# A retention gate by seven block products, head norms squared on ScalarE, tokens in turn through the up-projection, and a weight sum done by an adding DMA

## The reference, cut to what matters

```python
u = rmsnorm(h, norm_mix[l])
q, k, v, g_ret, p, gates = jnp.split(u @ w_in[l], split_points, axis=-1)
q, k = rotary(q), rotary(k) * 256 ** -0.5
ret = retention(q, k, v)                       # 4 heads of 256
ret = ret * lax.rsqrt(jnp.mean(ret * ret, axis=-1, keepdims=True) + NORM_EPS)
ret = ret.reshape(b, s, RET_V) * jax.nn.silu(g_ret)
pool_out = multiscale_pool(p, pool_w[l], pool_scale[l])
gate = jax.nn.sigmoid(gates.reshape(b, s, 2, D_MODEL) + gate_bias[l])
merged = gate[:, :, 0] * (ret @ w_ret_up[l]) + gate[:, :, 1] * (pool_out @ w_pool_up[l])
h = h + merged @ w_out[l]
```

## Time and profile before

| what | us |
|---|---|
| median of 3 runs | 1188.58 (1188.36 to 1188.71) |
| the profiled execution | 1188.89 |
| its span, first to last instruction | 1187.2 |
| TensorE busy in the span | 1177.9 (99%) |
| VectorE busy | 951.2 (80%) |
| ScalarE busy | 690.2 (58%) |
| GpSimd busy | 168.3 (14%) |

### The profile page before, as it was taken

The page is one execution under the profiler, slowest core; times in us unless marked ns, Lnnn a source line. Parts: engine busy times, 40 slices in busy tenths (PEclk is TensorE's granted clock), DMA queues, the critical chain, the costliest instruction groups (busy, mean ns, idle before and its releaser), DMA issues.

```text
span 1187.2 us, 14701 instructions
## 1 busy us (share of the span) xinstructions
PE 1177.9 (99%) x5704; PEld 976.9 (82%) x5704; DVE 951.2 (80%) x1158; ACT 690.2 (58%) x827; POOL 168.3 (14%) x170
## 2 busy tenths in 40 slices
PE   9999999999999999999999999999999999999997
PEld 8777888888888888888888888888899888888886
DVE  7788798878778798878788887569997766988884
ACT  7775656656547666554565555657562445566642
POOL 2100132210200132120031220000000100222200
PEclk9999999999999999999999999999999999999999
DMA  9434565447343555555455555652784344555540
GB/s 342 173 132 159 185 246 182 177 177 272 132 142 104 216 198 189 184 210 200 155 193 196 214 213 171 253 210 86 245 306 172 136 159 175 197 200 182 188 173 36
DMA packets 32872, 221.96 MB, mean 187 GB/s; under 512 B 3777, under 2 KB 4289, under 8 KB 7074
## 3 DMA queue, kind: packets, MB, share of 16 engines
q1 hardware_dynamic: 32514, 219.77, 51.4%
q0 software_dynamic: 144, 1.05, 0.5%
q10 hardware_dynamic: 144, 0.20, 0.0%
HBM read 219.95 MB, written 1.05 MB: 186 GB/s over the span
## 4 chain that ended last, share of the span: by engine, by line
PE 98%; issue 1%; DVE 1%; DMA 0%; ACT 0%; SPq 0%; POOLq 0%; POOL 0%; DVEq 0%; ACTq 0%
PE ps L305 30%; PE ps L307 30%; PE ps L306 30%; PE ps L310 5%; PE ps L313 3%; DMA raw<-in_w 0%; ACT whi L257 0%; DVE h L472 0%; DVE AR L2829 0%; DVE st L1878 0%; SPq L2851 0%; DVE AR L1896 0%; DVE AR L2477 0%; ACT whi L274 0%; ACT AR L2820 0%
## 5 line engine op out<-in xcount | busy, mean ns | idle before, releaser
L264 DVE SCALAR_TENSOR_TENSOR wlo<-raw,whi 128x2048 fp32r<-128x2048 f32 x164 | 375.2, 2295 | 75.7 <-ACT whi L257 48.4
L257 ACT CAST whi<-raw 128x2048 fp32r<-128x2048 f32 x166 | 317.7, 1916 | 172.0 <-PE ps L307 164.0
L305 PE MATMUL ps<-whi,xh 128*128 128x512 f32 x1000 | 394.3, 394 | 0.0
L307 PE MATMUL ps<-whi,xl 128*128 128x512 f32 x1000 | 389.8, 390 | 0.0
L306 PE MATMUL ps<-wlo,xh 128*128 128x512 f32 x1000 | 389.7, 390 | 0.0
L305 PEld LDWEIGHTS ps<-whi,xh 128*128 128x128 f32 x1000 | 187.7, 188 | 44.6 <-issue 1.6
L307 PEld LDWEIGHTS ps<-whi,xl 128*128 128x128 f32 x1000 | 187.7, 188 | 40.1
L306 PEld LDWEIGHTS ps<-wlo,xh 128*128 128x128 f32 x1000 | 187.9, 188 | 36.9
L305 PE MATMUL ps<-whi,yh 128*128 128x512 f32 x344 | 138.2, 402 | 0.0
L307 PE MATMUL ps<-whi,yl 128*128 128x512 f32 x344 | 134.4, 391 | 0.0
L306 PE MATMUL ps<-wlo,yh 128*128 128x512 f32 x344 | 134.0, 390 | 0.0
...
## 6 DMA issues: line engine op xcount, KB each, us to landing
raw<-in_w SPq DMA_DIRECT2D x198, 1024.0 KB, 4.8
...
AR<-in_b_pw SPq DMA_DIRECT2D x1, 1024.0 KB, 4.9
AR<-in_gate_bias SPq DMA_DIRECT2D x1, 1024.0 KB, 6.9
raw<-in_w POOLq DMA_DIRECT2D x1, 1024.0 KB, 8.2
...
```

What stands on the lines that cost most here:

```text
L257: e.copy(whi[:, v % S, :], raw_at(v)).then_inc(*sig.up("hi", v))
L264: e.scalar_tensor_tensor(out=wlo[:, v % S, :], in0=raw_at(v), scalar=1.0, in1=whi[:, v % S, :].bitcast(F32), op0=ALU.mult, op1=ALU.subtrac ...
L305: e.matmul(o, ah, bh, start=start, stop=False, skip_group_check=skip)
L307: return e.matmul(o, al, bh, start=False, stop=stop, skip_group_check=skip)
```

## The change

- The gate `gr` becomes a group like `v`: its units are seven in place of four, its banks ps4, ps5 and ps6, and its result (`KIND["gr"]`) lies where q and k lay. VectorE makes the first three sums of its weights; the fourth (unit gr + 5) is made by a DMA from GpSimd's queue that adds one slot of `raw` to another, and SyncE waits for it before it loads into the slot that is read.
- ScalarE reads the gate from SBUF, applies Silu in place, and VectorE scales by the norm and multiplies by the gate in one instruction for each head of 256 columns. `vector_ret_scale` goes.
- The squares of the head norms go from VectorE (two 512-wide squares and two sums for each j) to ScalarE (four 256-wide squares with a summing output for each j), right behind the copies to `vn`.
- The up-projection takes token tile 0 first for both halves of the columns (ps0, ps1), then tile 1 (ps4, ps5). The orders of all engines around are written anew.
- ScalarE's table for Silu is loaded earlier.

The diff, cut to its core (the first eight columns of indentation are left out):

```diff
 UNITS = {"sq": 2, "sk": 2, "sv": 2, "gqk": 2, "gv": 2, "gr": 2, "hout": 4, "ff0": 33, "pw1": 8, "pw2": 4, "ff1": 33,
-         "ffa": 33, "ret": 47, "ffb": 33}
+         "ffa": 33, "ret": 50, "ffb": 33}
 RET = {"p0": 2, "p1": 2, "g10": 2, "g11": 2, "pw": 1, "v": 7, "pu0": 2, "pu1": 2, "g0": 7, "q0": 2, "k0": 2,
-       "q1": 2, "k1": 2, "gr0": 2, "gr1": 2, "ru0": 2, "ru1": 2, "out": 4}
-GROUPS = ("v", "g0")
+       "q1": 2, "k1": 2, "gr": 7, "ru0": 2, "ru1": 2, "out": 4}
+GROUPS = ("v", "g0", "gr")
 ADDED = ("g0",)
...
 users = {}
-first_sum = ar(7680, UC)
+first_sum = {RU["v"]: ar(7680, UC), RU["g0"]: ar(7680, UC), RU["gr"]: ar(0, UC)}
 for v, n in enumerate(raw_of):
...
 def raw_at(v):
-    return first_sum if raw_of[v] is None else raw[:, raw_of[v] % R, :]
+    return first_sum[v - 1] if raw_of[v] is None else raw[:, raw_of[v] % R, :]
 
...
     if v in added_at:
+        return sig.at("added", v)
+    if v == RU["gr"] + 5:
         return sig.at("added", v)
...
 minus = st[:, 90:92]
-KIND = {"v": vn}
-GBANK = {"v": (4, 5, 6), "g0": (2, 3, 0), "g1": (4, 5, 2)}
+KIND = {"v": vn, "gr": ar(7680, 2, 1024)}
+GBANK = {"v": (4, 5, 6), "gr": (4, 5, 6), "g0": (2, 3, 0), "g1": (4, 5, 2)}
 DONE = {(0, 0): "y0", (0, 1): "z", (1, 0): "y1", (1, 1): "x"}
...
     q.wait_ge(*sig.at("summed", "minus"))
-    q.wait_ge(*banks.filled("pooled", 3))
+    q.wait_ge(*(banks.filled("sc", 3) if g == "gr" else banks.filled("pooled", 3)))
     e.activation(group_dst(g, t, j), ps[b][:, :], ACT.Copy, bias=0.0,
...
     q.wait_ge(*sig.at("gate_sig", 0, j, t))
-    e.tensor_tensor(s, ps[t][:, :], s, ALU.mult).then_inc(*banks.empty(f"ru{j}", t))
+    e.tensor_tensor(s, ps[banks.of[f"ru{j}", t]][:, :], s, ALU.mult).then_inc(*banks.empty(f"ru{j}", t))
     q.wait_ge(*banks.emptied(f"ru{j}", t))
...
                      scale=rstd[:, t:t + 1]).then_inc(*banks.empty("pv", t, j))
+    for t in range(2):
+        q.wait_ge(*banks.emptied("pv", t, j))
+        for n in range(2):
+            c = 512 * j + 256 * n
+            q.wait_ge(*sig.last("sumsq"))
+            e.activation(ar(5120, 256), vn[:, t, c:c + 256], ACT.Square, bias=0.0, scale=1.0 / 16,
+                         accum_out=ret_sums(j, t)[:, n:n + 1]).then_inc(*sig.up("sumsq", "ret", j, t, n))
 
...
 def vector_ret_norm(e, q, j):
-    squares = (ar(5120, 512), rota)
-    q.wait_ge(*sig.last("rotated"))
-    for t in range(2):
-        v = vn[:, t, 512 * j:512 * j + 512]
-        q.wait_ge(*banks.emptied("pv", t, j))
-        e.tensor_tensor(squares[t], v, v, ALU.mult).then_inc(*sig.up("v"))
-    q.wait_ge(*sig.last("v"))
-    for t in range(2):
-        e.tensor_reduce(ret_sums(j, t), squares[t].rearrange("p (h d) -> p h d", h=2), AXX, ALU.add).then_inc(*sig.up("v"))
-    q.wait_ge(*sig.last("v"))
     for t in range(2):
         s2 = ret_sums(j, t)
-        e.tensor_scalar(s2, s2, 1.0 / 256, EPS, ALU.mult, ALU.add).then_inc(*sig.up("ret_var", j, t))
-
-def vector_ret_scale(e, q, j, t):
-    v3 = vn[:, t, 512 * j:512 * j + 512].rearrange("p (h d) -> p h d", h=2)
-    q.wait_ge(*sig.at("ret_rstd", j, t))
-    e.tensor_tensor(v3, v3, ret_sums(j, t).unsqueeze(2).to_broadcast([P, 2, 256]), ALU.mult).then_inc(*sig.up("ret", j, t))
+        q.wait_ge(*sig.at("sumsq", "ret", j, t, 1))
+        e.tensor_scalar(s2, s2, EPS, None, ALU.add).then_inc(*sig.up("ret_var", j, t))
 
...
 def scalar_ret_gate(e, q, j, t):
-    q.wait_ge(*banks.filled(f"gr{j}", t))
-    if j or t:
-        q.wait_ge(*sig.at("gated", *((j, 0) if t else (j - 1, 1))))
-    q.wait_ge(*sig.at("rotated", "k1", 1, 1))
-    e.activation(gt, ps[4 + t][:, :], ACT.Silu, bias=0.0, scale=rstd[:, t:t + 1]).then_inc(*banks.empty(f"gr{j}", t))
+    g = group_dst("gr", t, j)
+    q.wait_ge(*group_done("gr", j, t))
+    e.activation(g, g, ACT.Silu, bias=0.0, scale=1.0).then_inc(*sig.up("gate_sig", "gr", j, t))
 
 def vector_ret_gate(e, q, j, t):
-    v = vn[:, t, 512 * j:512 * j + 512]
-    q.wait_ge(*banks.emptied(f"gr{j}", t))
-    q.wait_ge(*sig.at("ret", j, t))
-    e.tensor_tensor(v, v, gt, ALU.mult).then_inc(*sig.up("gated", j, t))
+    g = group_dst("gr", t, j)
+    q.wait_ge(*sig.at("gate_sig", "gr", j, t))
+    q.wait_ge(*sig.at("ret_rstd", j, t))
+    for n in range(2):
+        v = vn[:, t, 512 * j + 256 * n:512 * j + 256 * n + 256]
+        d = e.scalar_tensor_tensor(out=v, in0=v, scalar=ret_sums(j, t)[:, n:n + 1], in1=g[:, 256 * n:256 * n + 256],
+                                   op0=ALU.mult, op1=ALU.mult)
+    d.then_inc(*sig.up("gated", j, t))
 
...
             tensor_turned(e, q, "k1", RU["k1"], n, j)
-    quarter(e, q, "gr0", RU["gr0"], 0, 0, 4, xh, xl, x)
-    quarter(e, q, "gr0", RU["gr0"], 0, 1, 4, xh, xl, x)
-    quarter(e, q, "gr0", RU["gr0"], 1, 0, 5, xh, xl, x)
+    tensor_product(e, q, "gr", 0)
+    tensor_product(e, q, "gr", 1)
     tensor_ret_scores(e, q, 2)
     tensor_ret_scores(e, q, 3)
-    quarter(e, q, "gr0", RU["gr0"], 1, 1, 5, xh, xl, x)
+    tensor_product(e, q, "gr", 2)
+    tensor_product(e, q, "gr", 3)
     tensor_ret_values(e, q, 2)
     tensor_ret_values(e, q, 3)
-    quarter(e, q, "gr1", RU["gr1"], 0, 0, 4, xh, xl, x)
-    quarter(e, q, "gr1", RU["gr1"], 0, 1, 4, xh, xl, x)
+    tensor_product(e, q, "gr", 4)
     turn_x(e, q, "ret", None, 0, 0, vn[:, 0, :], "y", sig.at("gated", 0, 0))
-    quarter(e, q, "gr1", RU["gr1"], 1, 0, 5, xh, xl, x)
+    tensor_product(e, q, "gr", 5)
+    tensor_product(e, q, "gr", 6)
+    sig.alias("x_free", ("nm",), "made", ("gr", 6))
+    quarter(e, q, "ru0", RU["ru0"], 0, 0, 0, yh, yl, y_ret)
+    quarter(e, q, "ru1", RU["ru1"], 0, 0, 1, yh, yl, y_ret)
+    turn_x(e, q, "ret", None, 0, 1, vn[:, 0, :], "y", sig.at("gated", 1, 0))
+    quarter(e, q, "ru0", RU["ru0"], 0, 1, 0, yh, yl, y_ret)
     turn_x(e, q, "ret", None, 1, 0, vn[:, 1, :], "y", sig.at("gated", 0, 1))
-    quarter(e, q, "gr1", RU["gr1"], 1, 1, 5, xh, xl, x)
-    sig.alias("x_free", ("nm",), "full5", ("gr1", 1))
-    turn_x(e, q, "ret", None, 0, 1, vn[:, 0, :], "y", sig.at("gated", 1, 0))
-    quarter(e, q, "ru0", RU["ru0"], 0, 0, 0, yh, yl, y_ret)
-    quarter(e, q, "ru0", RU["ru0"], 0, 1, 0, yh, yl, y_ret)
+    quarter(e, q, "ru1", RU["ru1"], 0, 1, 1, yh, yl, y_ret)
     turn_x(e, q, "ret", None, 1, 1, vn[:, 1, :], "y", sig.at("gated", 1, 1))
-    quarter(e, q, "ru0", RU["ru0"], 1, 0, 1, yh, yl, y_ret)
-    quarter(e, q, "ru0", RU["ru0"], 1, 1, 1, yh, yl, y_ret)
-    quarter(e, q, "ru1", RU["ru1"], 0, 0, 0, yh, yl, y_ret)
-    quarter(e, q, "ru1", RU["ru1"], 0, 1, 0, yh, yl, y_ret)
+    quarter(e, q, "ru0", RU["ru0"], 1, 0, 4, yh, yl, y_ret)
+    quarter(e, q, "ru0", RU["ru0"], 1, 1, 4, yh, yl, y_ret)
     turn_x(e, q, "merge", None, 0, 0, merged[:, 0, :], "x", sig.at("merged", 0, 0))
-    quarter(e, q, "ru1", RU["ru1"], 1, 0, 1, yh, yl, y_ret)
-    quarter(e, q, "ru1", RU["ru1"], 1, 1, 1, yh, yl, y_ret)
+    quarter(e, q, "ru1", RU["ru1"], 1, 0, 5, yh, yl, y_ret)
     turn_x(e, q, "merge", None, 1, 0, merged[:, 1, :], "x", sig.at("merged", 0, 1))
-    sig.alias("y_free", ("ret",), "full1", ("ru1", 1))
+    quarter(e, q, "ru1", RU["ru1"], 1, 1, 5, yh, yl, y_ret)
+    sig.alias("y_free", ("ret",), "full5", ("ru1", 1))
     u = RU["out"]
...
     hi(e, q, RU["k0"] + 5)
+    e.preload_act_table_set("silu_and_others")
     hi(e, q, RU["q1"] + 4)
...
     hi(e, q, RU["k1"] + 5)
+    hi(e, q, RU["gr"] + 4)
+    scalar_part(e, q, "gr", 0)
+    scalar_part(e, q, "gr", 1)
+    hi(e, q, RU["gr"] + 5)
+    hi(e, q, RU["gr"] + 6)
     scalar_ret_gate(e, q, 0, 0)
-    hi(e, q, RU["gr0"] + 4)
-    scalar_ret_gate(e, q, 0, 1)
+    hi(e, q, RU["ru0"])
     scalar_ret_norm(e, q, 1)
-    hi(e, q, RU["gr0"] + 5)
+    scalar_part(e, q, "gr", 2)
+    split_turned_act(e, q, "y", "ret", 0, 0, yh, None, sig.at("y_free", "pool"))
+    hi(e, q, RU["ru0"] + 1)
     scalar_ret_gate(e, q, 1, 0)
-    split_turned_act(e, q, "y", "ret", 0, 0, yh, None, sig.at("y_free", "pool"))
+    hi(e, q, RU["ru1"])
+    scalar_part(e, q, "gr", 3)
+    hi(e, q, RU["ru1"] + 1)
+    split_turned_act(e, q, "y", "ret", 0, 1, yh)
+    for j in range(2):
+        scalar_ret_gate(e, q, j, 1)
     split_turned_act(e, q, "y", "ret", 1, 0, yh)
-    hi(e, q, RU["gr1"] + 4)
-    scalar_ret_gate(e, q, 1, 1)
-    split_turned_act(e, q, "y", "ret", 0, 1, yh)
-    hi(e, q, RU["gr1"] + 5)
     split_turned_act(e, q, "y", "ret", 1, 1, yh)
     hi(e, q, RU["ru0"] + 4)
+    split_turned_act(e, q, "x", "merge", 0, 0, xh, None, sig.at("x_free", "nm"))
     hi(e, q, RU["ru0"] + 5)
-    split_turned_act(e, q, "x", "merge", 0, 0, xh, None, sig.at("x_free", "nm"))
+    split_turned_act(e, q, "x", "merge", 1, 0, xh)
     hi(e, q, RU["ru1"] + 4)
-    split_turned_act(e, q, "x", "merge", 1, 0, xh)
     hi(e, q, RU["ru1"] + 5)
...
             lo(e, q, RU[key] + 4 + t)
+    vector_group_sum(e, q, "gr", 1)
+    vector_group_sum(e, q, "gr", 6)
     vector_ret_scores(e, q, 0)
...
     lo(e, q, RU["q1"] + 5)
+    vector_group_sum(e, q, "gr", 4)
     vector_ret_norm(e, q, 0)
```

(64 more changed lines are left out.)

## The result

| | before | changed |
|---|---|---|
| median of 16 runs, us | 1188.92 (1188.36 to 1189.38) | 1190.88 (1190.38 to 1192.58) |
| span of the profiled execution | 1187.2 | 1188.7 |
| TensorE busy, matmuls | 1177.9, 5704 | 1176.2, 5692 |

The ratio is 1.0019, with a 95% interval of 1.0012 to 1.0026: slower by 2.0 us, where 2.8 us were forecast. It lies in the range. It is slower than before beyond doubt, but just within the 0.2% that the text set as its bound for no change, so the forecast's own likeliest case (over 0.2%) was missed by a little.

A forecast was written before the change was run, and what follows sets the result against it. TensorE, busy 99% of the span, was taken as the bound. Saving -2.9, first wait +4.0 and second wait +1.7 sum to +2.8 us, 1191.4 us against the median of 1188.58; range 1189.0 to 1194.2 us.

The forecast's parts named there:

- the forecast's own likeliest case (over 0.2%): Whole kernel: slower than before by more than 0.2% (2.4 us), given a chance of 0.58.
- The bound and the saving: TensorE, busy 99%, bounds the kernel; the gate's 12 matmuls less and an old 0.20 us wait save 2.9 us.
- The second wait: TensorE's up-projection waits for the piece turned into ps7 just before, through ScalarE's rounding and VectorE's low part: 1.7 us.
- The first wait: TensorE's product 5 of the gate waits for ps6, holding the first turned piece, until ScalarE and VectorE finish: 4.0 us.
- Their last 3 us fall together ... I take 1.1: Adding DMA, overlapped by the next unit's plain load, lands 1.1 us later, at 935.9; 0 to 3.15 us possible.
- From there ScalarE has no gap: From the adding DMA's landing ScalarE works 10.9 us without idle time, so its rounding ends at 946.8.
- the text's lower end of 2.7 us: First wait if the adding DMA lands sooner: the copies to `vn` wait for values anyway, leaving 2.7 us.
- Two of the signs that the forecast named: ScalarE's cast after the adding DMA waits for it; the DMA lands 9 to 10 us after its issue.
- The rival on ScalarE being in time: Adding DMA lands before 934.6, squares are cheap; first wait 1.7 to 2.7 us, total 1189.6 us; chance 0.16.
- The rival on the clock: Idle time of some 4 us drops TensorE to 1.2 GHz; one block +5.5, total 1194.1 us; chance 0.10.
- No wait at all: Both TensorE waits together under 0.5 us, so the saving stands: 1185.7 us, faster; chance 0.10.
- A late add: The adding DMA with an SBUF source takes 11 us or more; at 11.4 us +4.9, total 1193.5 us; chance 0.10.

The follow-up runs named there:

- twelve_more: both_mended with 12 unread matmuls of 512 columns ahead of product 5 of the gate; 1188.80 us, ratio 0.9998 to the kernel before.
- other_bank: The changed kernel with the first turned piece sent to ps7, so product 5 of the gate (ps6) does not wait for it; 1188.06 us, ratio 0.9992.
- turn_early: The changed kernel with the second piece turned one quarter earlier and its gate made ahead of ru1's first low part; 1190.21 us, ratio 1.001.
- both_mended: The changed kernel with both the edits of other_bank and turn_early; 1186.36 us, ratio 0.9979 to the kernel before.
- add_late: The changed kernel with the adding DMA issued only after the low part of unit gr + 3 in place of gr + 2; 1199.29 us, ratio 1.0091.

## Why the prediction was right or wrong

- **The bound and the saving** were right. TensorE's starts, not durations, price a matmul; 12 matmuls less, and twelve_more gives 2.4 us by the medians and 2.76 by the profiles for them.
- **The place of both waits** was right, read from the order alone: a bank that is written again right behind a turn, and a piece that is read right behind its turn. other_bank and turn_early take away one each, and both_mended both.
- **The second wait** was right to 0.04 us. It is a chain with no queue in it.
- **The first wait** failed in its size, 2.4 us, not 4.0, and in what it waits for. The steps that failed are "Their last 3 us fall together ... I take 1.1", which put the landing at 935.9, and "From there ScalarE has no gap". The landing was at 933.75, 2.1 us sooner, and ScalarE had 0.84 us of gap behind it: the first wait hangs on the values, ready at 940.4, and on what ScalarE and VectorE do behind them, not on the adding DMA. Of the 2.1 us 1.1 are the plain load, which did not slow the add. In the changed kernel the load was issued at 929.74, but its first packet is at 932.88, when the add has only its last packets left, and the rate goes up only then:

```profile
930.00:931.00 1.00, 1.00 (x8) 0.91 (x7) 0.00 (x0) 0.00 (x0) 0.00 (x0) 1.00 1.01 205
931.00:932.00 1.00, 1.00 (x8) 0.90 (x7) 0.70 (x2) 0.00 (x0) 0.00 (x0) 1.00 1.16 172
932.00:933.00 1.00, 1.00 (x8) 0.92 (x7) 0.43 (x2) 0.39 (x1) 0.00 (x0) 1.00 0.87 98
933.00:934.00 1.00, 1.00 (x6) 0.81 (x5) 1.00 (x3) 1.00 (x3) 0.00 (x0) 1.00 0.92 377
```

  add_late shows that a load issued just ahead of it does delay it, by 3.2 us. In neither run did the two share the engines evenly: the packets that came first went first (though the load's took 5.1 us in add_late and 3.0 in the changed kernel). So the range was right and the choice of a third within it was not. 0.65 us came from an earlier low part and issue, 0.4 from the landing itself. With a landing off the path, the text's lower end of 2.7 us was the one that held; squares of 2.1 and not 2.4 us take off 0.3, and VectorE's addition ahead of the low part, which the forecast left out, gives back 0.2. Two of the signs that the forecast named did not come for this reason: the landing was not 9 to 10 us after the issue, and the cast did not wait for it.
- **The sum.** -2.93 + 2.41 + 1.66 = +1.1, and 1.9 was measured in the profile: 0.8 us are the small starts and the slightly slower matmuls named above, which I put at nothing. That the time came out at 1190.88, near the forecast's 1191.4, is in part luck: the first wait was set 1.6 us too long, these 0.8 us were left out, and the kernel before measured 0.3 us more than the median that I started from.
- **The rival on ScalarE being in time** (0.16) describes the first wait best; what it left out are these 0.8 us and the clock.
- **The rival on the clock** (0.10) was right as a mechanism and wrong in its price and its point. It needs no 4 us: 2.4 us did it, in some executions. A fall cost 1.7 us, not 2.7, in the one profile that has one behind a wait of 2.4 us. In the changed kernel, by the times, it hit 4 of 16, so the median hardly has it; its profile shows none. The page "TensorE: Matmul & The Clock Gate" of the Trainium skill (section "Part 1: The HAM clock gate") agrees with the trace in that idle time brings 1.2 GHz and work ends it.
- **No wait at all** (0.10) is excluded by the profile. **A late add** (0.10) is too, with 7.8 us; add_late made one of 11.0 us, and there each further us did count once the 1.1 us to spare were used up.
- The estimate by the page "DMA: Bandwidth & Descriptors" of the Trainium skill (section "Anatomy of one DMA — SWDGE (gpsimd) path"), 4.4 us for 1 MB, does not hold for an adding DMA: 7.8, 8.1 and 11.0 us were measured.
